# First scan of a two-block kernel: base copies ahead at a slot's boundary, and a norm one place later

## The reference, cut to what matters

```
def gated_delta_chunked(q, k, v, g, beta, s0):
    ...
    lower = jnp.where(strict, jnp.einsum('...id,...jd->...ij', k_beta, k) * decay, 0.0)
    a_mat = jnp.eye(CHUNK, dtype=jnp.float32) + lower
    sol = lax.linalg.triangular_solve(a_mat, rhs, left_side=True, lower=True, unit_diagonal=True)
    u, w = sol[..., :dv], sol[..., dv:]
    qk = jnp.where(incl, jnp.einsum('...id,...jd->...ij', q, k) * decay, 0.0)
    q_dec = q * jnp.exp(gc)[..., None]
    ...
    def step(s, inp):
        u_c, w_c, qk_c, qd_c, kd_c, ge_c = inp
        v_new = u_c - jnp.einsum('...ck,...kv->...cv', w_c, s)
        o_c = jnp.einsum('...ck,...kv->...cv', qd_c, s) + jnp.einsum('...ij,...jv->...iv', qk_c, v_new)
        s = s * ge_c[..., None, None] + jnp.einsum('...ck,...cv->...kv', kd_c, v_new)
        return s, o_c
```

## Time and profile before

| | us |
|---|---|
| median of 3 runs | 2619.45 (2618.48 to 2623.5) |
| the profiled execution | 2621.55 |
| its span | 2619.7 |
| PE busy | 2470.2 (94%) |
| DVE busy | 1424.4 (54%) |
| ACT busy | 1186.0 (45%) |
| POOL busy | 306.8 (12%) |
| mean granted clock of PE | 0.97 |

### The profile page before, as it was taken

The page is one execution under the profiler, slowest core; times in us unless marked ns, Lnnn a source line. Parts: engine busy times, 40 slices in busy tenths (PEclk is TensorE's granted clock), DMA queues, the critical chain, the costliest instruction groups (busy, mean ns, idle before and its releaser), DMA issues.

```text
span 2619.7 us, 52357 instructions
## 1 busy us (share of the span) xinstructions
PE 2470.2 (94%) x23199; PEld 2135.1 (82%) x23199; DVE 1424.4 (54%) x2229; ACT 1186.0 (45%) x1707; POOL 306.8 (12%) x425
## 2 busy tenths in 40 slices
PE   6999999999999999999999989899888889799998
PEld 6999888799999998878899965785477778678786
DVE  4654545466546645443666456445245540278885
ACT  4434466444444444564444355321254421167773
POOL 0100000021101100000311000641133321000000
PEclk8999999999999999999999989889899899899999
DMA  6754522256656644322566411101100004379993
GB/s 217 246 192 167 192 97 104 81 195 233 216 178 213 230 164 171 129 97 101 173 237 222 154 66 46 54 15 57 65 4 4 4 27 141 96 240 365 365 365 126
DMA packets 268884, 396.07 MB, mean 151 GB/s; under 512 B 9320, under 2 KB 172829, under 8 KB 268525
## 3 DMA queue, kind: packets, MB, share of 16 engines
q1 hardware_dynamic: 266921, 389.25, 43.4%
q0 software_dynamic: 1120, 2.17, 0.3%
q10 hardware_dynamic: 612, 1.24, 0.1%
HBM read 391.59 MB, written 1.05 MB: 150 GB/s over the span
## 4 chain that ended last, share of the span: by engine, by line
PE 75%; DVE 8%; issue 5%; DMA 5%; ACT 4%; POOL 2%; SPq 0%; ACTq 0%; DVEq 0%; POOLq 0%
PE ps L282 74%; DMA RB<-in_moe_w_up 5%; DVE gwl L431 2%; POOL H L1415 2%; ACT gwh L422 1%; POOL AR L2535 0%; ACT wh L422 0%; PE ps L1093 0%; DVE wl L431 0%; PE ps L520 0%; DVE AR L1677 0%; ACT AR L2752 0%; DMA RB<-in_ffn_w_gu 0%; ACT AR L2744 0%; DVE AT L1178 0%
## 5 line engine op out<-in xcount | busy, mean ns | idle before, releaser
L431 DVE TENSOR_TENSOR wl<-RB,wh 128x2048 fp32r<-128x2048 f32 (+4 forms) x188 | 412.5, 2197 | 294.5 <-ACT wh L422 293.9
L282 PE MATMUL ps<-H,RB 128*128 128x256 f32 (+1 forms) x1712 | 455.5, 423 | 1.1 <-ACT H L1515 1.1
L422 ACT ACTIVATE wh<-RB 128x2048 fp32r<-128x2048 f32 (+4 forms) x188 | 342.3, 1825 | 236.7 <-PE ps L282 205.3
L282 PEld LDWEIGHTS ps<-H,RB 128*128 128x128 f32 x1712 | 325.5, 193 | 115.1 <-issue 77.4
L282 PE MATMUL ps<-xhf,wl 128*128 128x256 f32 x1408 | 404.4, 287 | 14.0 <-DVE xlf L651 9.3
L282 PE MATMUL ps<-xlf,wh 128*128 128x256 f32 x1408 | 401.0, 285 | 0.0
L282 PE MATMUL ps<-xhf,wh 128*128 128x256 f32 x1408 | 400.8, 285 | 0.0
L282 PE MATMUL ps<-AR 64*64 64x64 f32 (+4 forms) x8296 | 276.1, 242 | 47.2 <-issue 19.7
L282 PEld LDWEIGHTS ps<-AR 64*64 64x64 f32 (+2 forms) x8296 | 241.9, 148 | 80.3 <-issue 51.0
L282 PEld LDWEIGHTS ps<-xhf,wl 128*128 128x128 f32 x1408 | 273.0, 194 | 24.9 <-DVE wl L431 14.8
L282 PEld LDWEIGHTS ps<-xlf,wh 128*128 128x128 f32 x1408 | 273.0, 194 | 0.1
(11 more groups left out here) (425 smaller groups left out, 4155.0 us busy)
## 6 DMA issues: line engine op xcount, KB each, us to landing
RB<-in_ffn_w_gu SPq DMA_DIRECT2D x88, 1024.0 KB, 7.7
RB<-in_w_in SPq DMA_DIRECT2D x25, 2048.0 KB, 7.7
RB<-in_ffn_w_down SPq DMA_DIRECT2D x16, 2048.0 KB, 7.8
RB<-in_w_gate SPq DMA_DIRECT2D x16, 2048.0 KB, 8.2
RB<-in_moe_w_gate SPq DMA_DIRECT2D x32, 1024.0 KB, 7.7
RB<-in_moe_w_up SPq DMA_DIRECT2D x32, 1024.0 KB, 10.2
RB<-in_moe_w_down SPq DMA_DIRECT2D x32, 1024.0 KB, 8.2
RB<-in_ada_w SPq DMA_DIRECT2D x12, 2048.0 KB, 9.9
```

What stands on the lines that cost most here:

```text
L282: return M.matmul(o, lhsT, rhs, start=start, stop=stop, skip_group_check=True)
L422: S.activation(self.pair(h)[0], of(slot_of(*key)), ACT.Copy).then_inc(*did("high", *mark))
L431: V.tensor_tensor(lo, of(slot_of(*key)), hi.bitcast(F32), ALU.subtract).then_inc(*did("low", *mark))
```

## The change

The order of the scan gets three moves, and the norm of the keys one:

- `form` of step n + 3 stands ahead of `mid` of level 5 (before: behind it).
- `out` and `state` of step n - 1 leave the place ahead of level 5 and stand behind `base_a` of the next slot (as `n - 3` there); those of step 5 stand behind the last slot.
- The two L2110 instructions become an entry of their own, `decay`, behind `more` of level 1 in slots 4 and 6, each with both steps' work.
- PE's sum of key column kj, and all that follows from it, stands in iteration kj + 6.

```
@@ gdn_order
             for n in range(0, 8, 2):
-                order += [("base_a", n, 0), ("base_b", n, 0), ("scale", n, 0)]
+                order += [("base_a", n, 0)]
+                order += [("out", n - 3, 0), ("state", n - 3, 0)] if n > 2 else []
+                order += [("base_b", n, 0), ("scale", n, 0)]
...
                 order += [("more", n, 1)]
+                order += [("decay", n, 0), ("decay", n + 1, 0)] if n > 3 else []
...
                 order += [("more", n, 4)]
-                order += [("out", n - 1, 0), ("state", n - 1, 0)] if n else []
-                order += [("mid", n, 5)]
                 order += [("form", n + 3, 0)] if n < 6 else []
-                order += [("more", n, 5)]
-            return order + [("apply", 6, 0), ("apply", 7, 0)]
+                order += [("mid", n, 5), ("more", n, 5)]
+            return order + [("out", 5, 0), ("state", 5, 0), ("apply", 6, 0), ("apply", 7, 0)]
@@ form_dve, and the new decay_dve
-                    for e in range(2):
-                        qe = u.QE.rearrange("p h (e c) n -> p e h c n", e=2)[:, e]
-                        ins = V.tensor_tensor(qe, qe, QT.rearrange("p (c h) n -> p h c n", h=2)[:, :, :, chunk(u, e)],
-                                              ALU.mult)
-                    ins.then_inc(*did("q_dec", u.n))
+
+            def decay_dve(u):
+                DV.wait_ge(*at("exp_g", u.n))
+                for e in range(2):
+                    qe = u.QE.rearrange("p h (e c) n -> p e h c n", e=2)[:, e]
+                    ins = V.tensor_tensor(qe, qe, QT.rearrange("p (c h) n -> p h c n", h=2)[:, :, :, chunk(u, e)],
+                                          ALU.mult)
+                ins.then_inc(*did("q_dec", u.n))
@@ shift_pe (shift_act and shift_dve alike)
-                    if 5 <= n < 9:
-                        kj = n - 5
+                    if 6 <= n < 10:
+                        kj = n - 6
```

More of the change, by code:

```diff
@@ L2261, in scan_dve @@
                         form_dve(u)
+                    elif what == "decay":
+                        decay_dve(u)
                     elif what == "base_a":
@@ L2475, in shift_act @@
                         ins.then_inc(*did("shift_pad", n))
-                    if 5 <= n < 9:
-                        root_act(f"kk{n - 5}", 512, 1.0, EPS[:, 0:1], KKR[:, (n - 5) % 2, :])
+                    if 6 <= n < 10:
+                        root_act(f"kk{n - 6}", 512, 1.0, EPS[:, 0:1], KKR[:, n % 2, :])
                     if n in (12, 14):
```

## The result

The changed kernel takes 2604.5 us in the median of five runs (2600.5 to 2608.5), the kernel before 2619.45: a ratio of 0.9939, with a 95% interval of 0.9927 to 0.9952, or 16 us less (13 to 19). The forecast was 2616.2 with a range down to 2611.5. The change is faster than the range allowed. The profiled execution has a span of 2602.8 us against 2619.7, 16.9 less.

What follows compares the result with a forecast made beforehand. PE works 94% of the span, so gains lie where it waits or runs at the lower clock. Terms -5.8, +1.0, -0.4, -0.45, +1.0, +1.45 sum to -3.2 us: 2619.45 to 2616.2, range 2611.5 to 2620.5.

Steps and rivals of the forecast that it cites:

- Shift stage: Shift stage: PE's two waits for ACT's square and the lower clock behind them go, less a new wait: -5.8 us net.
- Boundary 0/2: Boundary of slots 0 and 2: POOL's masks behind `form` delay level 5 and the base: +1.0 us, bounds 0 and +1.4.
- walk: Step-by-step timing of the engines' chain from POOL's masks through level 5 to PE's base at each slot boundary.
- Boundary 2/4, 4/6: The two later slot boundaries: DVE is free sooner but POOL's masks hold level 5: -0.4 and -0.45 us.
- Scan's end: End of scan: PE waits between the last two `apply` for DVE to read `state` of step 5: +1.0 us.
- Boundaries and end together: Sum of the scan's four waiting terms, three slot boundaries and the scan's end: +1.15 us.
- Clock: Slot boundaries: the lower clock may now fall ahead of level 5 instead of at the base: +1.45 us, bounds 0 and +3.5.
- The first rival: Clock stays up at one slot boundary; avoiding the last low stretch saves 4.3 us, giving 2612; chance 0.25.
- second case: The first rival: a boundary with less waiting keeps the higher clock; 2612, chance 0.25.
- The second and third rivals: Second: POOL's order and clock cost more than shift stage gives, 2622.3, chance 0.10. Third: shift-stage wait only moves, 2619, 0.12.

Runs made afterwards that it cites:

- restoring the end: Changed kernel with POOL's level 5 masks ahead of its `form`, and step 5's outputs and state back ahead of level 5 in the last slot: 0.9920 of the kernel before.
- second profile of the change: The changed kernel, unaltered, run once more on another chip beside the kernel before: 0.9954 of the kernel before, 12 us less.
- Masks first: Changed kernel with POOL's masks of level 5 put ahead of its part of `form` in slots 0, 2 and 4: 0.9929 of the kernel before.
- the scan alone: Changed kernel with its shift-stage part reversed, so only the scan's new order stays: 0.9978 of the kernel before, 5.8 us less.
- shift stage alone: Kernel before with only the change's shift stage, the scan's order as before: 0.9983 of the kernel before, 4.5 us less.
- last slot filled: Kernel before with three idle 128 x 512 products in PE's wait ahead of the base of slot 6 only: 0.9976 of the kernel before, 6.3 us less.
- five copies: Kernel with masks first and end restored, plus five extra DVE base copies ahead of the real one in slots 4 and 6: 0.9978 of the kernel before.
- form first: Kernel before with only `form` moved ahead of level 5: 0.9974 of the kernel before, 6.8 us less.
- state moved: Kernel before with only outputs and state of step n - 3 moved behind the base copies, `form` where it was: 0.9980 of the kernel before, 5.2 us less.
- two copies: Kernel with masks first and end restored, plus two extra DVE base copies ahead of the real one in slots 4 and 6: 0.9937 of the kernel before.

## Why the prediction was wrong, by its steps

| Term | Forecast, us | Measured, us |
|---|---|---|
| Shift stage | -5.8 | -6.4 in the profile; -4.5 (-7 to -1.8) alone |
| Boundary 0/2 | +1.0 | +1.3 at the base (walk: +1.4); PE's waits 1.46, now 1.92 |
| Boundary 2/4, 4/6 | -0.4, -0.45 | PE's wait 2.94, now 2.21 and 2.22 |
| Scan's end | +1.0 | a wait of 1.39; restoring the end took 1.1 us of idle time away |
| Boundaries and end together | +1.15 | idle time of the scan +0.6 |
| Clock | +1.45 | -11.2 |

**Right.** The shift stage went as walked: no wait for the square, products of 7.03 us, the low stretch of 3.4 us there gone, and 0.26 us ahead of `rv` where 0.35 were forecast. POOL's order holds level 5 back as walked, with waits of 0.97, 2.21 and 2.22 us where "about 2" stood, and L1613 below 1.3. From the first `mid` of level 5 to the base the walk had 3.70 us; at the boundary of slots 4 and 6 in the second profile of the change, where the clock stayed up, it is 3.55 (1721.58 to 1725.13). At the first boundary the base starts 31.2 us after the first base copy in the second profile of the change, which has the same low stretch inside slot 0 as before, against 29.9: +1.3, where the walk had +1.4. Masks first then showed that POOL is indeed what holds: without it 5.0 us of idle time went. The end's wait for `state`'s readers is 1.39 us, forecast 1.0 with an upper bound of 1.3.

**Wrong: the step "The clock".** The terms of the waits gave +1.15 for the scan, and its idle time grew by 0.6. Had the clock stayed as it was, the scan would have taken as long as before, and the total been some -6, inside the range. The step said: "it may now fall ahead of level 5 instead of at the base", priced the few pieces on which it falls anew, and kept in silence the long stretches behind the base. That is half of an account. It did fall on level 5, and from the first `mid` to the base it took 4.9 and 4.6 us in the first profile, where the walk had 3.7: 1.2 and 0.9 us, for which the step had 0.7 and took half. But the same sentence implies that it no longer falls at the base, and there before the change 30.7 us ran at the lower clock, 12.6 us of time by the 0.41. This was never written as a credit. With it the account closes: 10.2 and 13.7 us behind slots 4 and 6 are 9.8 us, 6.8 and 3.4 us around slots 2 and 0 are 4.2, less 2.8 for the two short stretches that are new: 11.2. The first of these, 9.8, is the order's by the runs above; of the 4.2 they don't show it.

The evidence stood in the earlier trace rows, which was read with the wrong question. I asked where the clock would fall next, and not how long it would stay down: 3.4 us ahead of the base, but 12.5 us and more behind the wait at the base, with 220 records of small matmuls in them. Once no boundary had one wait of 2.9 us, with as much idle time in the scan as ever, the long stretches didn't start, and with the wait made anew they were there at once.

**The first rival** had the right sign and a size too small: one stretch avoided, at 4.3 us, with a chance of 0.25. The last stretch alone is worth 5.64. Part of the gap is the price: 12.5 us were read where the stretch has 13.66, and the pace at the full clock, 9.0 us for 242 records, comes from a window that holds larger products too. The 160 records that took 4.88 us at the full clock would give 6.7 us for 220, so 5.8 for the loss. All three behind the boundaries went, in both profiles of the change. The evidence against it ("the matmuls of level 5 are few and small, and two waits stand close together") was an argument about whether the clock falls, while the money is in how long it stays down. The Trainium skill (TensorE: Matmul & The Clock Gate, "HAM oscillation — how this bites in real kernels") says that the drops repeat each time work waits anew between short pieces; its advice, to restructure so that they don't, was weighed as this rival (the prediction's "second case"). Here the trace sides with it, by 27.3 us of low clock less.

**The second and third rivals** have no row for them: the low stretches don't grow, and the shift's wait didn't move.

**Open.** Why one kernel has the same three short waits at two boundaries with a low stretch behind one of them only, and why the change itself had two short stretches in one profile and three in another at partly other places. But for the change each kernel has one profile here, so how often a stretch falls isn't known; the ratios, over many runs, carry the verdicts. The ratio of the scan alone (-5.8) is also smaller than the difference of its profile (-8.2), which would fit with stretches that vary from run to run, but that isn't shown. The kernel before itself goes from 2608.4 to 2624.8 us over 24 executions on one chip.

## What to carry to other kernels

Where stretches at the lower clock follow a wait, write them as a term of their own, with both sides: what the new place costs and what the old place gives back, at the price per us that two stretches of the same trace show (here 0.41 us for each us at the lower clock). A change that leaves the sum of the waits as it was but breaks or shortens the longest can be worth more than its idle time says: here the sum rose by 0.6 us and the scan fell by 10.6. If the order can't be changed, a few idle matmuls in the wait test the point within one run, and here they gave 10.5 us (7 to 14) where the new order of the scan alone gave 5.8 (2 to 9) on the same chip.

## What the runs showed of the hardware

- One wait of 2.94 to 3.00 us ahead of the 64x64 matmuls of a base had a long stretch at the lower clock that began around its end in each of the seven places where it occurs (before, shift stage alone, last slot filled, five copies): 10.2 us in slot 4, four times, and 13.7 us in slot 6, three times. Single waits of 1.3 to 1.6 us at the same places (form first, state moved, two copies) had none behind them in five of six, and 6.8 us in one. Single waits of 2.21 to 2.22 us ahead of the 64x64 matmuls of level 5 (the change twice, the scan's order alone) had 3.4 us around or behind their end in five of six places, none in one, and never more.
- The stretch of slot 6 is longer than that of slot 4 with the same wait, on different chips. In the kernel before it begins 0.98 us ahead of the base's first product, still in the wait, where that of slot 4 begins 0.66 us behind it. Neither needs the stretch at slot 2: with five late copies there is none, and the two are still 10.2 and 13.7. Whether that of slot 6 needs the one of slot 4 isn't shown.
- In the long stretches the 64x64 matmuls lost less than half: 0.40 to 0.41 us for each us at the lower clock (14.0 for 34.1, 10.9 for 27.3, 5.64 for 13.66), where work that follows the clock alone would lose 0.5.
